# A trunk of four feed-forward layers and two mixers in split fp32: how the feed-forward groups leave the banks, and how the last layer begins its output rows

## The chip, the cores and the metric

The kernel runs on one core of a Trainium2 chip (trn2). The metric is the device time of one launch in microseconds (us); 2278.42 us is the median of three runs of the kernel before. The engines are TensorE (PE; its weight loads are PEld), VectorE (DVE), ScalarE (ACT), GpSimd (POOL) and SyncE (SP), which here only issues DMAs.

## The reference

A decoder trunk over x of 512 tokens by 1024 features, float32:

```
for i in range(2):
    x = x + 0.5 * rmsnorm(swiglu(rmsnorm(x, ng[0]), ffn1_w_in[i], ffn1_w_out[i]), ng[1])
    h = rmsnorm(x, ng[2])
    m = hgrn2(h, ...) if i == 0 else gated_deltanet(h, ...)
    x = x + rmsnorm(m, ng[3])
    x = x + 0.5 * rmsnorm(swiglu(rmsnorm(x, ng[4]), ffn2_w_in[i], ffn2_w_out[i]), ng[5])

def swiglu(x, w_in, w_out):
    gate, up = split(x @ w_in, 2)          # w_in 1024 x 5632
    return (silu(gate) * up) @ w_out       # w_out 2816 x 1024
```

The change touches the four SwiGLU layers alone.

## The kernel before

Six sections run one after the other on all engines: `ffn`, `hg`, `ffn`, `ffn`, `gd`, `ffn`; `s` is the section's number and `LAST - 1` the last. Every large product is made of three TensorE passes: each operand is split into a high part in fp32r (ScalarE's copy) and the low rest (VectorE's subtraction of the high part from the original), and high x high, high x low and low x high are added up in a bank of PSUM. A weight block of 128 x 1024 (a "unit", 512 KB) is loaded by SyncE's queue into `raw`, `raw_more` or `raw_last`, split into `w_hi` (L783 `split`, L855 `weights_high`) and `w_lo` (L1472, L1588 `weights_low`), each a ring of four units, and used. `lo_split` and `unit_used` count the units.

**The plain part of a feed-forward layer.** The first 6 of its 22 feature tiles (`PLAIN`) are six pairs of one gate and one up unit, features by tokens. `pair(n)` scales both out of their banks (L1550, L1554), ScalarE takes the SiLU (L840), GpSimd multiplies (L2273) into `y_all`. Meanwhile VectorE makes from x seven combined moving operands (`factor_raw`: `norm`, `sums`), which ScalarE and VectorE split into `factor` (L850, L1583 `factor_low`).

**The groups.** The other 16 tiles are four groups (`QUADS`) of four, done by a scheme with seven products of half size instead of eight: products 1, 2 (`gates_early`, `gates_end`), 6 (`join`), 5 (`step`), 7 (`diff`), 4 (`rest`), 3 (`ups_early`), each of 2 units x 2 token tiles x 2 x 3 = 24 matmuls (L2537), tokens by features. Weight blocks of 5, 6, 4 and 7 are sums and differences of loaded ones (`step_sum` L1592, `join_sum` L1597, `rest_sum` L1601, `diff_sum` L1604). TensorE's order is 1, (4 and 3 of the group before), 2, 6, (turn of the group before), 5, 7. Banks 0, 1 hold products 1 and then 2 on top (`SUM_BANKS`), 2, 3 product 6 (`JOIN_BANKS`), 4, 7 product 7 and then 4 on top (`DIFF_BANKS`), 5, 6 product 5 and then 3 on top (`UP_BANKS`).

ScalarE copies product 1 out (`keep_first`, L892) before product 2 may be added. VectorE adds: `joins` (L1610), `late_ups` (L1620, L1623), `late_gates` (L1630), `early_ups` (L1635). ScalarE takes two SiLUs (`first_silu` L901, `late_silu` L906). GpSimd multiplies (`late_product` L2278, `early_product` L2283). TensorE transposes the four row tiles back (`turn`, L2598) and ScalarE drains them into `y_all` (`drain`, L912).

**The end of a layer.** All 22 feature tiles of y are split into `act_hi` (ScalarE, L921 `act_high`, L926 `last_high`) and `act_lo`: the first twelve by GpSimd (`BY_POOL = 12`, L2287), the others by VectorE (L1640). The last four come straight out of the turn's banks. The output projection (L2458) then goes over the tiles; in the last section it is written with tokens in rows (`row_block`, L2636), a block of weights being one feature tile, 128 x 1024, and the last group's turn and all of VectorE's lows stand before its first matmul. Its first units wait for `late_silu`, then the load of the table set (L988), then `split`.

**The last section** also needs x with tokens in rows at the very end. VectorE transposes it in 32 x 32 blocks (`turn(chunks)`, L1646), in three portions between the pairs; SyncE's queue writes it out in 32 DMAs of 64 KB (L678) behind the loads of units 12 to 15, and the loads for the groups (L661, L668) stand behind those. `x_turned` lies where `y_all` has its last tiles, so `keep_first` of group 0 waits for `x_rows_stored` (L890).

VectorE, ScalarE, GpSimd and SyncE each work in the order written here; they meet TensorE through counting semaphores only. The waits the text speaks of:

```
pe.wait_ge(dve_rows, diff_added(s, q, t))                      # rest: L2555
pe.wait_ge(act_rows, first_kept(s, q, t))                      # gates_end: L2565
pe.wait_ge(pool_rows, y_early(s, q, 1))                        # turn: L2590
pe.wait_ge(act_ready, (ffn_no[s] + 1) * (KF - BY_POOL))        # last section: L2630
```

## Time and profile before

| | us |
|---|---|
| median of three runs (2277.6 to 2283.09) | 2278.42 |
| the profiled execution | 2279.39 |
| its span | 2277.7 |
| TensorE busy | 2211.7 |
| VectorE busy | 1571.3 |
| ScalarE busy | 1146.8 |
| GpSimd busy | 462.6 |
| mean granted TensorE clock | 0.990 |

The span is from the first to the last instruction; the execution's own time also has what lies around it. A busy TensorE is not TensorE at its peak, since matmuls overlap: what a matmul costs is read from the distance of the starts. In a timeline a row gives start, duration, engine, line, operation, out and in, the number of instructions merged, and in brackets the idle time before it and what ended it. Neighbouring instructions of an engine overlap by about 0.1 us, so their distance is a little less than their duration. The first feed-forward section is over at about 377 us, the second begins near 655, the third ends at 1375, the last begins near 1909.

### The profile page before, as it was taken

The numbers are of one execution on the slowest core, as the hardware profiler recorded it, in microseconds if no ns is written. First come the engines' busy times: TensorE is split into PE (matmuls) and PEld (weight loads), VectorE is DVE, ScalarE is ACT, GpSimd is POOL, SyncE is SP. The second block draws the span as 40 slices with busy tenths as digits, with TensorE's granted clock in tenths as the row PEclk, the third lists the DMA queues.
The fourth block names the chain that finished last, engine by engine and source line by source line (L and its number), as shares of the span: only waits on it lengthen the run. The fifth ranks groups of instructions, "written<-read, shape, count | busy, mean of one in ns | idle before, by whom it ended". The sixth has DMA issues, their size and how long they took to land.

```text
span 2277.7 us, 30876 instructions
## 1 busy us (share of the span) xinstructions
PE 2211.7 (97%) x11642; PEld 1826.0 (80%) x11642; DVE 1571.3 (69%) x1886; ACT 1146.8 (50%) x1655; POOL 462.6 (20%) x343
## 2 busy tenths in 40 slices
PE   9999999999999999999999999999999999999899
PEld 7787788788787887887887887877788788788687
DVE  6998536777568897358988338877666726898723
ACT  5456435555544455344456336476666724445412
POOL 3025200101101144001116010123721110012500
PEclk9999999999999999999999999999999999999899
DMA  5322332222223323323321332221122132532321
GB/s 172 125 88 68 104 102 93 66 87 79 71 78 122 101 74 91 96 91 111 129 93 51 109 86 91 85 83 57 57 66 75 57 105 80 135 125 75 129 93 65
DMA packets 84766, 208.57 MB, mean 92 GB/s; under 512 B 25088, under 2 KB 29312, under 8 KB 84640
## 3 DMA queue, kind: packets, MB, share of 16 engines
q1 hardware_dynamic: 84112, 206.59, 28.9%
q8 instruction: 84, 1.38, 0.2%
q14 instruction: 42, 0.34, 0.0%
q10 hardware_dynamic: 528, 0.26, 0.0%
HBM read 202.56 MB, written 4.26 MB: 91 GB/s over the span
## 4 chain that ended last, share of the span: by engine, by line
PE 76%; DVE 14%; ACT 3%; issue 3%; POOL 2%; DMA 1%; SPq 1%; DVEq 0%; ACTq 0%; POOLq 0%
PE bank L2458 36%; PE bank L2537 17%; PE bank L2857 9%; PE bank L2636 5%; DVE w_lo L1588 3%; DVE w_lo L1472 2%; DVE h_lo L1477 1%; DVE raw L1601 1%; ACT w_hi L783 1%; PE bank L2598 1%; SPq L678 1%; DVE raw_more L1604 1%; POOL act_lo L2287 1%; ACT h_hi L795 1%; DMA raw_more<-in_ffn_in 1%
## 5 line engine op out<-in xcount | busy, mean ns | idle before, releaser
L1472 DVE TENSOR_TENSOR w_lo<-raw,w_hi 128x1024 fp32r<-128x1024 f32 x283 | 362.4, 1293 | 434.4 <-ACT w_hi L783 434.3
L2537 PE MATMUL bank<-w_hi,factor 128*128 128x512 f32 x1792 | 557.9, 392 | 23.2 <-DVE w_lo L1588 12.4
L783 ACT ACTIVATE w_hi<-raw 128x1024 fp32r<-128x1024 f32 x283 | 293.9, 1054 | 285.1 <-PE bank L2458 188.8
L2537 PEld LDWEIGHTS bank<-w_hi,factor 128*128 128x128 f32 x1792 | 334.8, 189 | 101.7 <-issue 16.7
L2537 PE MATMUL bank<-w_lo,factor 128*128 128x512 f32 x896 | 350.0, 391 | 0.0
L2458 PE MATMUL bank<-h_hi,w_hi 128*128 128x512 f32 (+1 forms) x775 | 296.0, 382 | 7.8 <-DVE v_fm L1783 2.9
L2458 PE MATMUL bank<-h_hi,w_lo 128*128 128x512 f32 (+1 forms) x775 | 285.5, 368 | 0.0
L2458 PE MATMUL bank<-h_lo,w_hi 128*128 128x512 f32 (+1 forms) x748 | 275.3, 368 | 0.0
L2458 PE MATMUL bank<-act_hi,w_hi 128*128 128x512 f32 (+1 forms) x594 | 218.3, 367 | 5.2 <-DVE w_lo L1472 5.2
L2458 PE MATMUL bank<-act_hi,w_lo 128*128 128x512 f32 (+1 forms) x594 | 217.2, 366 | 0.0
L2458 PE MATMUL bank<-act_lo,w_hi 128*128 128x512 f32 (+1 forms) x594 | 217.1, 365 | 0.0
L2537 PEld LDWEIGHTS bank<-w_lo,factor 128*128 128x128 f32 x896 | 168.8, 188 | 35.8
L2458 PEld LDWEIGHTS bank<-h_hi,w_hi 128*128 128x128 f32 x775 | 146.6, 189 | 39.4 <-issue 8.5
L2458 PEld LDWEIGHTS bank<-h_hi,w_lo 128*128 128x128 f32 x775 | 146.6, 189 | 24.7
L2458 PEld LDWEIGHTS bank<-h_lo,w_hi 128*128 128x128 f32 x748 | 141.7, 189 | 24.6 <-issue 2.6
L2857 PE MATMUL bank<-h_hi,w_hi 128*128 128x512 f32 x360 | 150.9, 419 | 1.2 <-DVE conv_in L1883 0.7
L2857 PE MATMUL bank<-h_hi,w_lo 128*128 128x512 f32 x360 | 148.7, 413 | 0.0
L2857 PE MATMUL bank<-h_lo,w_hi 128*128 128x512 f32 x360 | 148.0, 411 | 0.0
L2458 PEld LDWEIGHTS bank<-act_hi,w_hi 128*128 128x128 f32 x594 | 112.1, 189 | 24.4 <-DVE w_lo L1472 6.4
L2458 PEld LDWEIGHTS bank<-act_lo,w_hi 128*128 128x128 f32 x594 | 112.1, 189 | 18.1
L2458 PEld LDWEIGHTS bank<-act_hi,w_lo 128*128 128x128 f32 x594 | 112.0, 189 | 18.1
L855 ACT ACTIVATE w_hi<-raw_more 128x1024 fp32r<-128x1024 f32 x80 | 84.8, 1060 | 73.5 <-PE bank L2537 36.8
(358 smaller groups left out, 4019.8 us busy)
## 6 DMA issues: line engine op xcount, KB each, us to landing
raw<-in_ffn_in SPq DMA_DIRECT2D x84, 512.0 KB, 3.7
raw<-in_gd_in SPq DMA_DIRECT2D x49, 512.0 KB, 3.6
raw_more<-in_ffn_in SPq DMA_DIRECT2D x48, 512.0 KB, 3.8
raw_last<-in_ffn_in SPq DMA_DIRECT2D x40, 512.0 KB, 4.9
raw<-in_ffn_out SPq DMA_DIRECT2D x48, 384.0 KB, 3.1
raw<-in_hg_in SPq DMA_DIRECT2D x32, 512.0 KB, 3.7
raw<-in_ffn_out SPq DMA_DIRECT2D x48, 320.0 KB, 2.9
raw<-in_last_out SPq DMA_DIRECT2D x22, 512.0 KB, 3.6
```

The costliest lines, as they stand in the source:

```text
L678: sp.dma_start(dst[:, c], src[:, c]).then_inc(x_rows_stored, 16)
L783: nc.scalar.activation(w_hi[:, u[0] % RING, :], raw[:, u[0] % RING, :], ACT.Copy).then_inc(hi_split, 1)
L795: nc.scalar.activation(h_hi[:, c, half(h)], x[:, c, half(h)], ACT.Copy, scale=pre_gain(s, c)).then_inc(h_hi_ready, 1)
L855: nc.scalar.activation(w_hi[:, u % RING, :], place, ACT.Copy).then_inc(hi_split, 1)
L1472: nc.vector.tensor_tensor(w_lo[:, r, :], raw[:, r, :], w_hi[:, r, :].bitcast(f32), ALU.subtract).then_inc(lo_split, 1)
L1477: nc.vector.scalar_tensor_tensor(out=h_lo[:, c, half(h)], in0=x[:, c, half(h)], scalar=pre_gain(s, c), in1=h_hi[:, c, half(h)].bitcast(f32 ...
L1588: TT(w_lo[:, u % RING, :], place, w_hi[:, u % RING, :].bitcast(f32), ALU.subtract).then_inc(lo_split, 1)
L1601: TT(lower_gate_place(s, q, a), lower_gate_place(s, q, a), join_place(s, q, a), ALU.subtract).then_inc(joint_made, 1)
L2458: ins = nc.tensor.matmul(dst[:, half(h)], w, moving[ml][:, k, :][:, half(h)], start=first and n == 0 and (wl, ml) == (0, 0), stop=last and ...
L2537: ins = nc.tensor.matmul(bank[dst[t]][:], factor[:, 2 * i + ml, at:at + P], (w_hi, w_lo)[wl][:, u % RING, b * TOK:(b + 1) * TOK], start=st ...
L2636: ins = nc.tensor.matmul(bank[tok_bank(t, h)][:], (act_hi, act_lo)[ml][:, k, t * P:(t + 1) * P], (w_hi, w_lo)[wl][:, r, half_row(h)], star ...
L2857: ins = MM(bank[unit_bank(n)][:], (w_hi, w_lo)[wl][:, (u0 + n) % RING, k * P:(k + 1) * P], (h_hi, h_lo)[ml][:, k, :], start=x == 0, stop=x ...
```

## The change

- `y` of the plain tiles is split soon after it is made: ScalarE's `act_high` in the pairs and after `keep_first` of group 0, the lows (`act_low`) by VectorE between its pairs and groups. GpSimd makes no lows. `ActHighs` and `ActLows` find each tile's place.
- The turned tiles of group 2 are split out of the banks (`turned_high`, `turned_low`) and no longer drained; those of group 3 as before.
- Product 4 goes into banks 2, 3 as a product of its own and waits for `joins`; `late_ups` writes its first sum to `late_gate`, where `late_gates` adds product 4.
- Product 1 of group 0 runs both units for token tile 0, then both for tile 1; `keep_first` copies tile 0 after the first half.
- VectorE's factor lows 2 to 6 move: 2 behind `pair(5)`, 3 between the two w_lo of product 6, 4 before w_lo(7,0), 5 and 6 behind w_lo(7,1).
- The last group's early product is VectorE's (`last_rows`).
- Last section: x is transposed before `pair(0)`, stored between the loads of units 11 and 12; the wait for the stores stands in `drain` of group 0. The output rows begin with token tile 2 for the first four weight blocks, then comes the turn, then tiles 0, 1 and 3 of the same blocks.

The diff's core (counters that only number the new order, and the SBUF layout, are left out):

```diff
 SyncE, last section
-                for n in range(0 if s else RING, N_PLAIN):
+                for n in range(0 if s else RING, 2 * PLAIN):
                     load((u0 + n, 0), weights(row0 + n))
                 if s == LAST - 1:
-                    for a in range(P // SUB):
-                        sp.wait_ge(turned, KD)
...
+                    for c in range(KD):
+                        sp.wait_ge(turned, c + 1)
+                        for a in range(P // SUB):
...
                             sp.dma_start(dst[:, c], src[:, c]).then_inc(x_rows_stored, 16)
+                for n in range(2 * PLAIN, N_PLAIN):
+                    load((u0 + n, 0), weights(row0 + n))
 ScalarE
 (pair)
+                    if n:
+                        act_high(n - 1)
 (keep_first)
-                    act.wait_ge(unit_used, unit_of(s, q, 1) + 2)
                     if q:
+                        act.wait_ge(unit_used, unit_of(s, q, 1) + 2)
                         act.wait_ge(dve_rows, join_made(s, q - 1, 1))
-                    elif s == LAST - 1:
-                        act.wait_ge(x_rows_stored, 16 * 4 * KD)
+                    else:
+                        act.wait_ge(y_turned, first_halves(s))
                     for t in range(2):
+                        if t and q == 0:
+                            act.wait_ge(unit_used, unit_of(s, q, 1) + 2)
 (drain)
+                    if s == LAST - 1 and q == 0 and fs[0] == 0:
+                        act.wait_ge(x_rows_stored, 16 * 4 * KD)
+                def turned_high(q, f):
+                    last = q == QUADS - 1
+                    act.wait_ge(unit_used, unit_of(s, QUADS - 1, 4 if last else 2) + 2)
+                    act.wait_ge(y_turned, turned_by(s, q, f))
+                    src = bank[(*DIFF_BANKS, *(JOIN_BANKS if last else SUM_BANKS))[f]]
+                    nc.scalar.activation(high_rows(PLAIN + 4 * q + f), src[:], ACT.Copy).then_inc(act_hi_ready, 1)
 (groups)
                     diff_weights(q, 0)
                     if last:
+                        turned_high(q - 1, 0)
+                        turned_high(q - 1, 1)
...
                     diff_weights(q, 1)
+                    if last:
+                        turned_high(q - 1, 2)
+                        turned_high(q - 1, 3)
...
-                for k in range(5, 10):
+                for k in range(PLAIN, PLAIN + 2):
                     act_high(k)
                 rest_weights(q, 0)
...
 VectorE
-                        TT(late_rows(t), bank[DIFF_BANKS[t]][:], sq[:, t, :], ALU.add).then_inc(dve_rows, 1)
+                        TT(late_gate(t), bank[DIFF_BANKS[t]][:], sq[:, t, :], ALU.add).then_inc(dve_rows, 1)
...
-                        TT(late_gate(t), bank[DIFF_BANKS[t]][:], sq[:, t, :], ALU.add).then_inc(dve_rows, 1)
+                        TT(late_gate(t), bank[JOIN_BANKS[t]][:], late_gate(t), ALU.add).then_inc(dve_rows, 1)
+                def last_rows():
+                    for t in range(2):
+                        dve.wait_ge(dve_rows, up_early(s, QUADS - 1, t))
+                        dve.wait_ge(act_rows, silu_first(s, QUADS - 1, t))
+                        TT(y_first[:, t, :], y_first[:, t, :], y[:, t, :], ALU.mult).then_inc(dve_rows, 1)
+                def turned_low(q, f):
+                    k = PLAIN + 4 * q + f
+                    src = bank[(*DIFF_BANKS, *(JOIN_BANKS if q == QUADS - 1 else SUM_BANKS))[f]]
+                    dve.wait_ge(act_hi_ready, act_count(s, k))
+                    TT(low_rows(k), src[:], high_rows(k).bitcast(f32), ALU.subtract).then_inc(act_ready, 1)
+                if s == LAST - 1:
+                    dve.wait_ge(x_ready, N_ITEMS * s)
+                    dve.wait_ge(acc_done, POOLED * (2 * s + 1))
+                    for c in range(KD):
+                        nc.vector.transpose(x_turned[:, c, :], x[:, c, :]).then_inc(turned, 1)
...
                     sums()
+                act_low(0)
                 pair(4, 0)
                 factor_low(0)
                 factor_low(1)
+                act_low(1)
+                pair(5, 2)
                 factor_low(2)
-                pair(5, 2)
 (group q, from w_lo(6,0) on)
                     weights_low(q, 6, 0, join_place(s, q, 0))
                     if q:
                         early_ups(q - 1)
+                    else:
+                        factor_low(3)
                     weights_low(q, 6, 1, join_place(s, q, 1))
...
                     weights_low(q, 5, 1, gate_place(s, q, 1))
                     if q == 0:
-                        for i in range(4, FACTORS):
-                            factor_low(i)
+                        factor_low(4)
+                    else:
+                        act_low(q + 2)
                     weights_low(q, 7, 0, up_place(0))
-                    joins(q)
+                    if last:
+                        turned_low(q - 1, 0)
+                        turned_low(q - 1, 1)
+                    if q:
+                        joins(q)
                     weights_low(q, 7, 1, up_place(1))
+                    if q == 0:
+                        factor_low(5)
+                        factor_low(6)
+                        joins(0)
+                        act_low(2)
                 q = QUADS - 1
+                turned_low(q - 1, 2)
+                turned_low(q - 1, 3)
                 weights_low(q, 4, 0, lower_gate_place(s, q, 0))
+                weights_low(q, 4, 1, lower_gate_place(s, q, 1))
                 late_ups(q)
-                weights_low(q, 4, 1, lower_gate_place(s, q, 1))
-                act_low(BY_POOL)
                 weights_low(q, 3, 0, lower_up_place(s, q, 0))
                 weights_low(q, 3, 1, lower_up_place(s, q, 1))
-                act_low(BY_POOL + 1)
+                for k in range(PLAIN, PLAIN + 4):
+                    act_low(k)
                 late_gates(q)
-                act_low(BY_POOL + 2)
-                act_low(BY_POOL + 3)
+                act_low(PLAIN + 4)
+                act_low(PLAIN + 5)
                 split((v0, 0))
+                act_low(PLAIN + 6)
+                act_low(PLAIN + 7)
                 early_ups(q)
                 split((v0 + 1, 0))
-                act_low(BY_POOL + 4)
-                act_low(BY_POOL + 5)
+                last_rows()
                 split((v0 + 2, 0))
                 split((v0 + 3, 0))
-                for k in range(KF - 4, KF):
-                    act_low(k)
+                for f in range(4):
+                    turned_low(q, f)
 GpSimd
-                for k in range(BY_POOL):
-                    act_low(k)
                 for t in range(2):
                     late_product(QUADS - 1, t)
-                for t in range(2):
-                    early_product(QUADS - 1, t)
 TensorE
 (product)
+                    if (q, p) == (0, 1):
+                        quarter(0, 0)
+                        quarter(1, 0).then_inc(y_turned, 1)
+                        for a in range(2):
+                            quarter(a, 1).then_inc(unit_used, 1)
+                        return
 (rest)
-                        pe.wait_ge(dve_rows, diff_added(s, q, t))
-                    product(q, 4, DIFF_BANKS, free, False)
+                        pe.wait_ge(dve_rows, join_made(s, q, t))
+                    product(q, 4, JOIN_BANKS, free, True)
 (diff, free)
+                        if q == QUADS - 1:
+                            pe.wait_ge(act_ready, act_count(s, KF - 8 + t))
 (last section)
-                turn(QUADS - 1)
-                pe.wait_ge(act_ready, (ffn_no[s] + 1) * (KF - BY_POOL))
-                for k in range(KF - RING):
+                for k in range(RING):
+                    pe.wait_ge(lo_split, v0 + k + 1 + SKEW)
+                    ready(k)
+                    for h in range(2):
+                        row_block(k, 2, h)
+                turn(QUADS - 1)
+                for t in range(2):
+                    pe.wait_ge(dve_rows, up_early(s, QUADS - 1, t))
+                    pe.wait_ge(act_ready, act_count(s, KF - 4 + t))
+                    for k in range(RING):
+                        for h in range(2):
+                            row_block(k, t, h)
+                pe.wait_ge(act_ready, act_count(s, KF - 1))
+                for k in range(RING):
+                    for h in range(2):
+                        ins = row_block(k, 3, h)
+                    ins.then_inc(unit_used, 1)
+                for k in range(RING, KF - RING):
```

## Rows read from the trace of the kernel before

**Rows 1.** The page's first part: busy us (share), instructions.

```profile
PE 2211.7 (97%) x11642; PEld 1826.0 (80%) x11642; DVE 1571.3 (69%) x1886; ACT 1146.8 (50%) x1655; POOL 462.6 (20%) x343
```

**Rows 2.** The chain that ended last, in order of time: start, us, what.

```profile
98.28 32.89 PE bank L2537 x144
```

**Rows 3.** TensorE's waits: total us, times, longest.

```profile
PE bank L2537 <- DVE w_lo L1588: 12.4, 16, 1.1
PE bank L2458 <- DVE w_lo L1472: 6.6, 7, 1.7
PE bank L2598 <- POOL y_first L2283: 6.0, 1, 6.0
PE bank L2537 <- ACT y_all L892: 6.0, 4, 3.7
PE bank L2537 <- DVE gate L1620: 3.7, 4, 0.9
```

**Rows 4.** Timeline of TensorE, first section's last group.

```profile
212.40 0.70 PE L2537 MATMUL bank<-w_hi,factor 128*128 128x512 f32 x2
...
216.21 0.73 PE L2537 MATMUL bank<-w_hi,factor 128*128 128x512 f32 x2 [0.80 <-DVE w_lo L1588]
...
225.59 0.70 PE L2537 MATMUL bank<-w_hi,factor 128*128 128x512 f32 x2 [0.93 <-DVE gate L1620]
...
232.94 0.73 PE L2537 MATMUL bank<-w_hi,factor 128*128 128x512 f32 x2 [0.92 <-DVE w_lo L1588]
...
240.40 0.50 PE L2458 MATMUL bank<-act_hi,w_hi 128*128 128x512 f32 x1 [1.72 <-DVE w_lo L1472]
```

**Rows 5.** Timeline of VectorE, same stretch.

```profile
213.84 4.55 DVE L1588 TENSOR_TENSOR w_lo<-raw_more,w_hi 128x1024 fp32r<-128x1024 f32 x2
218.32 1.28 DVE L1610 TENSOR_TENSOR sq<-bank,y_all 128x512 f32<-128x512 f32 x2
...
234.54 0.68 DVE L1630 TENSOR_TENSOR acc<-bank,sq 128x512 f32<-128x512 f32 x1
```

**Rows 6.** Timeline of GpSimd, same stretch.

```profile
208.33 23.47 POOL L2287 TENSOR_TENSOR act_lo<-y_all,act_hi 128x512 fp32r<-128x512 f32 x12
```

**Rows 7.** Timeline of ScalarE, same stretch.

```profile
236.50 1.28 ACT L988 ACT_TABLE_LOAD   x1
```

**Rows 8.** Timeline of VectorE, section at 655: groups 0 and 1.

```profile
728.37 1.22 DVE L1588 TENSOR_TENSOR w_lo<-raw,w_hi 128x1024 fp32r<-128x1024 f32 x1
...
731.77 3.50 DVE L1583 TENSOR_TENSOR factor<-factor_raw,factor 128x1024 fp32r<-128x1024 f32 x3
...
767.96 1.21 DVE L1588 TENSOR_TENSOR w_lo<-raw_more,w_hi 128x1024 fp32r<-128x1024 f32 x1
```

**Rows 9.** Timeline of TensorE, section at 655, group 0.

```profile
719.00 0.70 PE L2537 MATMUL bank<-w_hi,factor 128*128 128x512 f32 x2 [0.78 <-ACT y_all L892]
...
736.55 0.69 PE L2537 MATMUL bank<-w_hi,factor 128*128 128x512 f32 x2 [0.95 <-DVE w_lo L1588]
```

**Rows 10.** Timeline of SyncE's queue, last section.

```profile
1953.57 19.64 SPq L678 DMA_DIRECT2D x_rows<-x_turned  x32
```

**Rows 11.** Timeline of TensorE, last section, group 0.

```profile
1975.43 1.19 PE L2537 MATMUL bank<-w_hi,factor 128*128 128x512 f32 x2 [3.66 <-ACT y_all L892]
...
1997.34 0.70 PE L2537 MATMUL bank<-w_hi,factor 128*128 128x512 f32 x2 [1.11 <-DVE w_lo L1588]
```

**Rows 12.** Timeline of VectorE, last section, pairs.

```profile
1927.59 0.69 DVE L1550 TENSOR_TENSOR gate<-bank,rms 128x512 f32<-128x512 f32 x1 [0.45 <-ACT rms L790]
...
1935.78 1.89 DVE L1646 STREAM_TRANSPOSE x_turned<-resid 128x512 f32<-128x512 f32 x3
```

**Rows 13.** Timeline of TensorE, last section: turn and first rows.

```profile
2143.80 0.66 PE L2598 MATMUL bank<-ident,y_first 128*128 128x128 f32 x2 [6.03 <-POOL y_first L2283]
...
2149.53 0.79 PE L2636 MATMUL bank<-w_hi,act_hi 128*128 128x512 f32 x1 [2.08 <-DVE act_lo L1640]
```

**Rows 14.** Busy time by stretch: us, busy of each engine, TensorE's granted clock, DMA share, GB/s.

```profile
2149.50:2155.20 5.70, 5.67 (x14) 4.47 (x15) 0.00 (x0) 0.00 (x0) 0.00 (x0) 0.51 0.80 281
```

169 lines of the change are left out of this document (85 added, 84 removed).

## Prediction

> **What bounds the kernel now.** I read the page's first part, then TensorE's waits, then the timelines of each engine around the longest of these waits, and the chain that ended last for the pace. TensorE is busy for 97% of the span and nothing else comes near it [rows 1], so only its idle time and its slow stretches can be won: the change leaves every matmul in. The chain gives 144 matmuls of six products in 32.89 us [rows 2], so a product of 24 takes about 5.45 us, one matmul 0.227 us. TensorE's waits that concern the feed-forward code are five kinds, together 34.7 us (a few of the 6.6 us lie elsewhere) [rows 3]: a lower split of a weight block, the kept copy of the first product, an addition read out of the banks (`gate`, L1620), and in the last layer the turn behind GpSimd's `y_first`. The last layer also loses time with no wait: after 3.66 us of idleness, and again after the idle stretch before 2149.5, matmuls start at about half their rate; from 2149.5 to 2155.2 the granted clock is 0.51, the 1.2 GHz level, and 14 matmuls run where 25 would fit [rows 11, 14].
>
> The profiled execution took 2279.39 us (span 2277.7 and 1.7 around it), 1 us above the median 2278.42. I sum against 2279.39.
>
> **Closing stretch of a feed-forward layer (four times).** I take the first layer's; the others repeat it within 0.2 us. From the first matmul of the last group's product 5 at 212.40 to the first of the output projection at 240.40 pass 28.0 us, where four products need 21.8. The holes are before products' halves at 216.21, 225.59, 232.94 and at 240.40 [rows 4], with a smaller one between.
>
> Their cause is VectorE. While GpSimd computes, a 128x1024 subtraction of two SBUF operands takes 2.3 us; with GpSimd idle the same instruction takes 1.21 us, 1.13 from start to start [rows 5, 6, 8]. GpSimd's twelve `act_low` fill 23.5 us from 208.33 on [rows 6]. The change deletes them there. VectorE gets the twelve: at 0.60 us from start to start (the addition at 234.54, 0.68 with 0.08 of overlap [rows 5]; half of a 1.13 us one gives 0.57) that is 7.2 us, and 1.2 us for `last_rows`, which replaces the last `early_product`. Not all of it is in this stretch: lows 0 to 2 go into the pairs and group 0, lows 3, 4 and 5 into groups 1, 2 and 3. GpSimd's products for group 2 remain and run until 208.33, where the lows begin [rows 6], so relief starts there.
>
> I lay VectorE's new order out from that point, 1.13 for 1024 and 0.60 for 512 columns: diff sum 0 ends 208.9, w_lo(5,0) 210.0, diff sum 1 211.2, w_lo(5,1) 212.3, act_low(5) 212.9, w_lo(7,0) 214.0, two `turned_low` 215.2, joins 216.4, w_lo(7,1) 217.6, two `turned_low` 218.8, w_lo(4,0) 219.9, w_lo(4,1) 221.0. ScalarE must give the highs first: turn of group 2 begins at 210.7, so turned highs 0, 1 lie at 211.4 to 212.4, w_hi(7,1) 213.4, highs 2, 3 214.4; none is late. TensorE, from 212.5, wants (5,1) at 215.2, (7,0) 218.0, (7,1) 220.7, (4,0) 223.4, (4,1) 226.1: all are there, with 2.9 us or more in hand. So the hole at 216.21 goes. The fourth product writes bank 2, 3 and waits for the join additions (216.4), not for the additions that read banks 4 and 7, so the hole at 225.59 goes. Product 7 ends at 223.4; `late_ups` takes 2.4 us to 226.0, w_lo(3,0) 227.1, w_lo(3,1) 228.3, wanted at 228.9 and 231.6. The hole at 232.94 goes too. Product 3 ends at 234.3.
>
> What is late next: the output projection's first weight block. Its chain is late_gates, late_silu, the table load, w_hi, w_lo. Before, it took 5.86 us from 234.54 to 240.40 [rows 4, 5, 7]. It now starts when four act_lows (6 to 9) are done: 228.3 + 2.4 = 230.7, so the projection starts at 236.5 and TensorE waits 2.2 us for it. Gain 240.4 - 236.5 = 3.9 us. Its second block is wanted 4.1 us later, at 240.6; VectorE has two lows, `early_ups` and a split before it, 240.0. In three layers, 3 x 3.9 = **11.7 us**.
>
> The Trainium skill (SBUF — State Buffer, "Who interferes with whom") says that VectorE with two SBUF inputs contends with a GpSimd instruction that reads SBUF, one holding the port for its whole instruction, and that with one SBUF input it doesn't. By that rule alone the sum above holds and the rival "slower" below is out, while without it 2306 us stays possible. The trace agrees: the additions out of a bank at 218.32 take 0.6 us each while GpSimd works, and the 1024-wide ones before them twice their time [rows 5].
>
> **First group (four times).** The first product in order of token tiles lets ScalarE copy tile 0 2.7 us earlier, and gates_end no longer waits: 0.94 us at 719.00 [rows 9]. It is given back at once. Factor low 3 now stands before w_lo(6,1), so w_lo(5,0), which ended 729.6, ends 730.7 [rows 8], while TensorE (join held to 723.9 by w_lo(6,0)) is ready at 729.4: a new wait of 1.4 us. Product 5 then ends at 736.3. The wait at 736.55 [rows 9] goes, since one factor low stands before w_lo(7,0) instead of three (3.5 us) [rows 8]; it ends 735.3. Product 7 starts 736.35 instead of 736.55. Behind it stand factor lows 5, 6, the joins, act_low(2), then the next group's first w_lo at 741.6, wanted 741.8: just in time. Gain 0.2 us; bounds -1.2 (w_lo late by another instruction) and +2.0 (both holes gone). Four times: **0.6 us**, rounded down. The act_low in groups 1 and 2 cost nothing: there the block that it precedes is ready 4 us before TensorE wants it.
>
> **Last layer, first group.** Before, 32 stores of 64 KB took SyncE's queue 19.64 us from 1953.57, 0.61 each, and the kept copy waited for them to land [rows 3, 10]; the loads of up and lower_up stood behind them. From the first product (1975.43 - 3.8 - 5.45 = 1966.2) to product 7 at 1997.34 [rows 11] are 31.1 us; the layer at 719 needs 712.6 to 736.55, 23.9. So 7.2 us are lost, slow clock included. Now eight transposes (0.60 each from 1.89 for three, less overlap [rows 12], 4.8 in all) run before pair(0), and the 32 stores go from 1927.7 to about 1947.4, between load 11 and load 12. Loads 12 and 13 are wanted at 1959, 14 and 15 can't start before 1952 as now; the quarters find an empty queue. The wait for the stores moves to `drain`, 70 us later. The price: pair(0) starts at 1931.9 instead of 1927.59 [rows 12] (transposes can't begin before the gathers and splits end, 1927.1); gate, silu and gate again, 0.68, 0.7 and 0.7, make gate(1) ready at 1934.05; TensorE's unit 6 needs it and starts at 1966.2 - 6 x 5.45 = 1933.5, so it slips 0.6 us. Gain 7.2 - 0.6 = **6.6 us**.
>
> **Last layer, end.** Before, product 3 ended, TensorE idled 6.0 us to 2143.80 for y_first, turned at half clock, idled 2.08 us, and lost 5.7 x 0.49 = 2.7 us in the slow stretch behind 2149.5: as if the rows had begun at full speed at 2152.2 [rows 13, 14]. Now the shared part brings product 3's end to 234.3 + 1899.1 = 2133.4. Then four blocks of token tile 2, 1.36 us each, run as VectorE delivers them. In the first layer's times: block 0 at 236.5; w_lo 1 after two lows, early_ups and the split, 240.0; last_rows to 241.2; w_lo 2 242.3, w_lo 3 243.5. TensorE idles 2.2, 2.2 and 0.95 us, turns 245.2 to 247.0, and goes on with tile 0 after 0.1. Rows' full-speed equivalent: 234.3 + 5.35 + 1.75 + 0.4 = 241.8, that is 2140.9. Gain 2152.2 - 2140.9 = **11.3 us**.
>
> Sum: 11.7 + 0.6 + 6.6 + 11.3 = 30.2, so 2279.39 - 30.2 = **2249 us**.
>
> **Rivals.** *Clock.* The three idle stretches at the last layer's end lie between bursts of 1.36 us. After 3.66 us idle the clock fell to 1.2 GHz, after 1.72 us in the middle of work it didn't [rows 4, 11]; these are between. If it falls, the turn's 1.75 us may take half as long again and the slow stretch costs 2.7 [rows 14]: 2252.5. The Trainium skill (TensorE: Matmul & The Clock Gate, "What's actually happening") has the clock follow how busy the engine has recently been; this speaks against cutting the start into bursts.
>
> *Queues tie up.* turned_low waits for ScalarE, ScalarE for the turn, and w_lo(7,1) and w_lo(4,0) stand behind it. If turn or ScalarE is 3 us later than laid out, each layer gets back two holes of about 1 us, and the last layer's blocks 1 us: 2249 + 9 = 2258. Slack of 2.9 us speaks against it.
>
> *Stores do not hide.* They share the queue with loads 12 to 15; should those be late by as much as the stores took beyond my estimate, the 6.6 us are lost: 2256.
>
> *Slower.* GpSimd isn't what slows VectorE. Then the doubled times stay: nine and a half 1024-wide instructions of 1.13 us more and five lows of 1.2 more, less 2.5 us of slack, put late_gates 14.1 us later than laid out, so each layer's projection starts 14.1 - 3.9 = 10.2 us later than before. The last layer's own terms (6.6, and 11.3 - 3.9 = 7.4) remain: 2279.4 + 41 - 14 = 2306. Linear between the two, it decides once the instruction takes over 1.13 + 1.14 x 30.2 / 57 = 1.73 us. Against it: 1.21 us at 767.96, same line, with GpSimd idle [rows 8].
>
> **How the numbers follow.** As worked 0.55 (alone 2245 to 2253); clock 0.15; queues 0.13; stores 0.05; slower 0.04; the rest split: better than worked (first-group holes both gone) 0.06, none of it 0.02. The range 2242 to 2263 reaches from the better case, 4 x 1.8 us below, past queues and stores with some of both. 0.3% is 6.8 us, about what a measurement can tell. Faster 0.92, same 0.03, slower 0.05.
>
> **What would show it.** Right: VectorE's w_lo at 1.2 us in the last group; no hole in products 5, 7, 4, 3; 2.2 us before the projection; 1.4 us before product 5 of group 0; no 3.7 us wait near 1971; two or three waits under 2.5 us at L2636. Wrong: w_lo still at 2.3, waits inside products 4 or 3, or a clock of 0.5 at the rows' start.

## Result and the profile after

The kernel after takes 2256.27 us (median of 4 runs, 2255.43 to 2257.03) where the kernel before took 2278.01: the ratio is 0.990, 95% interval 0.9883 to 0.9917, 22 us less. 2249 was forecast; the time lies inside the range, 7 us above the forecast. The profiled executions are 2279.39 and 2256.88 us, 22.5 apart, and everything below is worked out between them.

The page's first part, for [rows 1]:

```profile
PE 2199.7 (98%) x11642; PEld 1819.9 (81%) x11642; DVE 1549.6 (69%) x1942; ACT 1139.2 (51%) x1639; POOL 366.1 (16%) x287
```

TensorE's waits (us in total, times, longest), for [rows 3]:

```profile
PE bank L2514 <- DVE w_lo L1515: 8.3, 7, 2.3
PE bank L2703 <- DVE w_lo L1515: 4.9, 3, 2.3
PE bank L2593 <- DVE w_lo L1631: 4.6, 4, 1.2
PE bank L2668 <- POOL y_first L2347: 4.1, 3, 1.4
PE bank L2593 <- issue: 3.9, 4, 1.1
```

The kept copy and `gate` are gone from the list, and the sixteen waits for weight lows inside products are four. New are `y_first` before the first turn three times, and four waits in the products for nothing the profile names, where before had one. The first section's timeline of TensorE, every hole over 0.15 us, and at 215.48 the first matmul of the last group's product 5, for [rows 4]:

```profile
87.46 0.70 PE L2593 MATMUL bank<-w_hi,factor 128*128 128x512 f32 x2 [0.93 <-issue]
...
94.32 0.70 PE L2593 MATMUL bank<-w_hi,factor 128*128 128x512 f32 x2 [1.13 <-DVE w_lo L1631]
...
134.03 0.41 PE L2668 MATMUL bank<-ident,y_first 128*128 128x128 f32 x2 [1.35 <-POOL y_first L2347]
...
215.48 0.71 PE L2593 MATMUL bank<-w_hi,factor 128*128 128x512 f32 x2
...
239.79 0.74 PE L2514 MATMUL bank<-act_lo,w_hi 128*128 128x512 f32 x2 [2.29 <-DVE w_lo L1515]
```

Between the last two lines lie products 5, 7, 4 and 3 without a hole, 24.3 us where [rows 4] had 28.0. A hole in this text is the distance of two starts less the 0.23 us of a matmul; the brackets, which count from a modelled end, show about 0.15 us less (2.29 for a hole of 2.44). The last section ends so, for [rows 13]:

```profile
2124.19 0.73 PE L2703 MATMUL bank<-w_hi,act_lo 128*128 128x512 f32 x2 [2.29 <-DVE w_lo L1515]
...
2127.72 0.73 PE L2703 MATMUL bank<-w_hi,act_lo 128*128 128x512 f32 x2 [1.88 <-DVE w_lo L1515]
...
2130.06 0.73 PE L2703 MATMUL bank<-w_hi,act_lo 128*128 128x512 f32 x2 [0.70 <-DVE w_lo L1515]
...
2135.08 0.70 PE L2703 MATMUL bank<-w_hi,act_lo 128*128 128x512 f32 x2 [0.25 <-DVE act_late L1692]
```

To compare kernels part by part I counted matmuls: a feed-forward section's grouped part is the same number of them in every kernel here, so the time from the start of one to the start of another can be set side by side. "Group 0" is the first 120, "to turn 0" the next 120 (group 1 up to its turn), "closing" the last 96 (products 5, 7, 4, 3) up to the first projection matmul. "Second series" is experiment 5. At 0.2266 us a matmul they would take 27.2, 27.2 and 21.8 us. The four columns of each are the four sections, us; where the last turn comes ahead of the rows (before, and last turn first), the last section's closing reaches up to that turn:

```
kernel (profiled run)   group 0                    to turn 0                  closing
before                  29.31 29.49 29.60 36.73    27.21 27.21 27.21 27.21    28.00 28.01 27.99 32.30
after                   29.83 29.95 29.71 29.95    28.71 27.23 28.75 28.73    24.31 24.31 24.31 24.33
after, second series    29.10 29.39 29.21 29.12    27.26 28.76 28.71 27.26    24.34 24.34 24.34 24.34
product 4's bank back   29.65 29.15 29.11 29.08    28.75 28.75 28.76 27.26    24.36 24.36 24.36 24.36
GpSimd busy             29.88 29.86 29.94 29.30    27.24 27.23 28.72 27.23    28.87 28.85 28.83 28.98
stores late             30.22 29.17 29.34 36.60    27.23 28.75 28.73 28.73    24.34 24.34 24.34 24.34
last turn first         29.14 29.15 29.16 29.08    27.26 28.72 27.26 27.26    24.31 24.34 24.34 29.17
products on VectorE     29.65 29.95 29.22 29.75    27.21 27.23 27.22 27.24    24.30 24.31 24.31 24.33
weights split early     29.79 29.74 29.10 29.18    27.25 27.23 28.73 27.24    21.89 21.86 21.89 21.89
group 0's order         27.20 27.25 27.20 28.24    27.21 27.21 27.21 27.26    24.34 24.31 24.31 24.34
all orders              27.20 27.21 27.65 28.27    27.21 27.21 27.24 27.22    21.89 21.86 21.86 21.89
all, and products       27.20 27.23 27.96 28.28    27.21 27.21 27.26 27.23    21.86 21.86 21.86 21.89
all, bank back          27.20 27.23 27.23 28.22    27.21 27.21 27.26 27.25    23.05 23.07 23.07 23.08
all, last rows' order   27.33 27.25 27.23 28.24    28.71 27.21 27.22 27.26    21.89 21.86 21.86 21.89
```

### The profile page after: what moved, and what is told of

Read it like the earlier page. It is cut to its first block, busy times and chain, and to the rows that moved or that the text cites. A ratio compares the mean times of both kernels' runs of the same rounds, so it can differ in the third digit from the quotient of the medians.

```text
span 2255.2 us, 30953 instructions
## 1 busy us (share of the span) xinstructions
PE 2199.7 (98%) x11642; PEld 1819.9 (81%) x11642; DVE 1549.6 (69%) x1942; ACT 1139.2 (51%) x1639; POOL 366.1 (16%) x287
## 3 DMA queue, kind: packets, MB, share of 16 engines
q1 hardware_dynamic: 84112, 206.59, 29.4%
## 4 chain that ended last, share of the span: by engine, by line
PE 78%; DVE 10%; issue 5%; ACT 3%; POOL 2%; DMA 2%; SPq 0%; DVEq 0%; ACTq 0%; POOLq 0%
PE bank L2514 37%; PE bank L2593 18%; PE bank L2941 9%; PE bank L2703 5%; DVE w_lo L1515 2%; DVE w_lo L1631 1%; PE bank L2668 1%; DMA raw_more<-in_ffn_in 1%; DVE h_lo L1520 1%; ACT w_hi L821 1%; ACT h_hi L833 1%; DVE resid L1550 1%; PE bank L3103 1%; PE bank L3082 1%; PE bank L3110 1%
## 5 line engine op out<-in xcount | busy, mean ns | idle before, releaser
L2514 PE MATMUL bank<-act_late,w_hi 128*128 128x512 f32 (+1 forms) x648 | 200.7, 367 | 0.0
L2514 PE MATMUL bank<-act_lo,w_hi 128*128 128x512 f32 (+1 forms) x540 | 171.2, 368 | 6.9 <-DVE w_lo L1515 6.9
L2514 PE MATMUL bank<-act_late,w_lo 128*128 128x512 f32 (+1 forms) x432 | 158.0, 366 | 0.0
L2514 PEld LDWEIGHTS bank<-act_late,w_hi 128*128 128x128 f32 x648 | 118.8, 189 | 19.7
L2514 PEld LDWEIGHTS bank<-act_lo,w_hi 128*128 128x128 f32 x540 | 100.0, 190 | 24.9 <-DVE w_lo L1515 8.1
L1631 DVE TENSOR_TENSOR w_lo<-raw_more,w_hi 128x1024 fp32r<-128x1024 f32 x80 | 100.5, 1268 | 20.6 <-ACT w_hi L895 20.6
```

The lines of the kernel that those rows point to most:

```text
L1631: TT(w_lo[:, u % RING, :], place, w_hi[:, u % RING, :].bitcast(f32), ALU.subtract).then_inc(lo_split, 1)
L2514: ins = nc.tensor.matmul(dst[:, half(h)], w, moving[ml][:, k, :][:, half(h)], start=first and n == 0 and (wl, ml) == (0, 0), stop=last and ...
```

## The experiments

Twelve runs, one of them the kernel after again; each edit is to the kernel after unless it says otherwise, and the cuts shown leave out what only follows from them. Experiments 1 to 4 are compared with 2256.27 us, experiments 6 to 10 with the second series' 2256.62, experiments 11 and 12 with experiment 9. The kernel before took 2278.5 us beside the second series and 2278.9 beside experiment 9.

**1. Product 4 back on the difference's banks.**

```diff
-                        pe.wait_ge(dve_rows, join_made(s, q, t))
-                    product(q, 4, JOIN_BANKS, free, True)
+                        pe.wait_ge(dve_rows, diff_added(s, q, t))
+                    product(q, 4, DIFF_BANKS, free, False)
...
-                            pe.wait_ge(dve_rows, gate_late(s, q - 1, t))
+                            pe.wait_ge(dve_rows, join_made(s, q - 1, t))
```

> The kernel after, with its fourth product put back on the difference's banks (product 4 adds onto what product 7 left in banks 4 and 7, and the join's product waits for the step before it as in the kernel before); all else stays. Theory (the bank of its own removes a wait of TensorE in the last group of each section, where product 4 stood ready and VectorE had not yet added the difference): the hole ahead of product 4 in the last group comes back at about 1.1 us in each of four sections, and the time is 2260.5, 4.2 us over the kernel after. Rival A (the hole had gone because VectorE is no longer slowed by GpSimd there, and the bank does nothing): within 1 us of the kernel after. Rival B (the additions of the difference now stand ahead of what joins wait for in every group, so that holes come in groups 2 and 3 too): 2265 or more.

2252.78 us (2251.17 to 2256.93), ratio 0.9885 (0.987 to 0.990). TensorE, at product 4 and at the projection:

```profile
226.45 0.70 PE L2595 MATMUL bank<-w_hi,factor 128*128 128x512 f32 x2 [0.93 <-DVE gate L1663]
...
238.72 0.73 PE L2516 MATMUL bank<-act_lo,w_hi 128*128 128x512 f32 x2 [1.12 <-DVE w_lo L1515]
```

The hole came back where the theory had it, and the projection's fell from 2.44 us to 1.28: the closing stretch is the same to 0.05 us. All three expectations missed the time. In the kernel after the bank only moves a microsecond, because the projection's first weight low ends when it ends.

**2. GpSimd kept busy in the last group.** 22 subtractions that nothing reads:

```diff
+                pool.wait_ge(dve_rows, gate_late(s, QUADS - 2, 1))
+                for n in range(22):
+                    pool.wait_ge(pool_rows, POOL_ROWS * ffn_no[s] + 18 + n)
+                    nc.gpsimd.tensor_tensor(idle_rows[:], x[:, 0, 0:2 * P], x[:, 1, 0:2 * P], ALU.subtract).then_inc(pool_rows, 1)
                 for t in range(2):
                     late_product(QUADS - 1, t)
```

> The kernel after, with GpSimd kept busy in the last group of each section: 22 subtractions of 128x256 that nothing reads, about where the kernel before had its twelve lows (some 20 us); they leave nothing out of the computation. Theory (in the kernel before it was GpSimd's traffic in SBUF that drew VectorE's weight lows from 1.2 to 2.3 us in this stretch, and VectorE's lateness that made TensorE wait): VectorE's instructions of 128x1024 on SBUF come back to about 2.3 us each while GpSimd runs, holes ahead of products 5, 7 and 4 come back, and the time is 2260 to 2262. Rival A (the lows' cost was the wait of the projection for GpSimd's own results, not its traffic): no change, within 1 us of 2256.3. Rival B (a 256 wide instruction gives VectorE its turn twice as often, so the slowing is half): VectorE's come to 1.6 to 1.8 us, holes under 0.5 us, 2257 to 2258.

2277.89 us (2274.82 to 2280.69): 21.6 us more, the whole gain of the change. GpSimd, VectorE and TensorE in the first section, then the stretch behind (us, busy time of each engine, granted clock):

```profile
208.13 29.40 POOL L2360 TENSOR_TENSOR idle_rows<-resid 128x256 f32<-128x256 f32 x22
```

```profile
210.68 1.76 DVE L1632 TENSOR_TENSOR w_lo<-raw_more,w_hi 128x1024 fp32r<-128x1024 f32 x1
```

```profile
242.01 0.80 PE L2519 MATMUL bank<-act_lo,w_hi 128*128 128x512 f32 x1 [5.91 <-DVE w_lo L1516]
```

```profile
242.00:246.00 4.00, 3.99 (x9) 3.14 (x10) 4.00 (x6) 1.22 (x2) 0.00 (x0) 0.50 0.34 98
```

VectorE's instructions go from 1.21 to 1.76 us, which is what rival B said of them (a narrower GpSimd instruction delays less than the 2.3 us beside one of 512), and the loss is far over the theory's: 4.5 us in each closing stretch, 18.3 in all, and TensorE's clock at its 1.2 GHz level behind the hole. My 4 to 6 us was the cost of one section. The load is also longer than the lows of before were (29.4 us, not 23.5), and late products queue behind it, so this isn't the old kernel. But VectorE has no idle stretch from 204.5 to 239.7 in the first section, so it is late by its slower instructions alone: GpSimd's traffic is enough to take the gain away. The prediction had put the point where nothing is left of the gain of the new order at 1.73 us an instruction; here it is 1.76.

**3. The last layer's stores late**, transposes in three portions, stores behind all loads, and the copy waiting for them, as before:

```diff
+                turn(range(0, 3))
                 pair(2, 5)
...
+                        if s == LAST - 1:
+                            act.wait_ge(x_rows_stored, 16 * 4 * KD)
```

> The kernel after, with the last layer's transposes of x and their stores as in the kernel before: transposes in three portions between the first pairs, the 32 stores on SP behind all its weight loads, and ScalarE's copy of the first product's result waiting for all of them. Theory (that chain was what held up the last layer's first group): a hole of about 7 us comes back in that group, the time is 2262.9, 6.6 us over the kernel after. Rival (the early transposes now cost nearly as much where they stand, ahead of the first pair, so undoing them gives half of it back): 2259 to 2260.

2261.22 us (2260.4 to 2261.87), 4.9 more. TensorE in the last section's group 0:

```profile
1966.30 0.70 PE L2599 MATMUL bank<-w_hi,factor 128*128 128x512 f32 x2 [3.36 <-ACT y_all L934]
...
1976.11 0.70 PE L2599 MATMUL bank<-w_hi,factor 128*128 128x512 f32 x2 [2.47 <-issue]
```

The median lies between the theory's 2262.9 and the rival's 2260; the stretch itself is clear. Group 0 goes from 29.95 to 36.60 us, 6.65 as the theory says; the second hole is the join, whose loads stood behind the stores. The 0.5 us ahead of the pairs comes off. The rest of the difference between 6.1 and 4.9 is of the size in which the second series of the kernel after differs from its first in group 0.

**4. The last turn first**, then all rows: `turn(QUADS - 1)` and a wait for all 22 lows ahead of the row blocks.

> The kernel after, with the last projection in the order of before: the last turn first, then a wait for all 22 highs and lows, then all rows tile by tile, instead of tile 2 of the first four rows ahead of the turn. Theory (the order hides the chain of product, turn, copy and low behind 16 row blocks): TensorE's idle time between its last product and steady rows grows from 5.6 us to 8.5 to 12, the time is 2259.1 if its clock doesn't fall and 2262.7 if it falls to half for a stretch. Rival (the chain isn't hidden in the kernel after either, its holes of 2.44, 2.04, 0.86 and 0.30 us being the same chain in parts): within 1 us of 2256.3.

2260.35 us (2252.88 to 2261.59), 4.1 more.

```profile
2124.76 0.66 PE L2668 MATMUL bank<-ident,y_first 128*128 128x128 f32 x2 [7.12 <-DVE y_first L1682]
...
2129.84 0.73 PE L2703 MATMUL bank<-w_hi,act_lo 128*128 128x512 f32 x2 [1.47 <-DVE act_late L1692]
```

Two holes of 7.28 and 1.62 us in place of 5.64 in four: the new order of the rows is worth 3.3 us of holes, as the theory says. With the clock, which fell to its 1.2 GHz level at 2121.4 here, it is 4.5: the last section takes 159.8 us from the last group's product 5 to the end, not 155.3. The medians alone don't show it, as the two intervals overlap (ratio 0.9895 to 0.9924 here, 0.9883 to 0.9917 for the kernel after).

**5. The kernel after again.**

> The kernel after itself, unchanged, timed beside the next three kernels on their chip. It says how far a few holes of 1 us and a few falls of TensorE's clock carry a kernel from one series to another. Theory (the kernel with product 4 back on the difference's banks was no faster than the kernel after, its 3.5 us being startup and clock falls that come in some executions and not in others): the ratio to before lies between 0.9885 and 0.9905, the time at 2254 to 2257. Rival (the bank of its own costs time): 2256.3 again, ratio 0.990 or more.

2256.62 us (2255.05 to 2258.29), ratio 0.9904 (0.9888 to 0.992). Both expectations hold this result, so it doesn't choose between them. The interval overlaps that of experiment 1, so whether the shared bank is 3 us better in this kernel stays undecided; experiment 11 asks it again where it can be seen. The table shows what changes from one execution to the next: group 0 by up to 0.8 us, and the turn's 1.5 us, which is there in other sections now.

**6. GpSimd's products of groups 0 to 2 on VectorE.**

```diff
                     weights_low(q, 6, 1, join_place(s, q, 1))
+                    if q:
+                        products(q - 1)
                     rest_sum(q, 0)
```

> The kernel after, with the twelve products of gate and up rows per section that GpSimd did in groups 0 to 2 on VectorE (4 more instructions of 128x512 in SBUF in a group, some 0.68 us each by VectorE's low of that size), in the place behind the low of the join's second quarter. Theory (the hole of 1.5 us ahead of the first group's turn comes from GpSimd and VectorE competing for SBUF, which starves one of them): all turn holes go (3 to 4 of them, 1.5 us each, 4.6 to 6 us), no VectorE instruction of 128x1024 in groups 1 to 3 takes over 1.3 us, and the time is 2251. Rival A (VectorE is full there, and its four more products push the lows that TensorE waits for): holes of 1 to 2 us ahead of product 5 or 7 in nine groups, 2260 or more. Rival B (the turn waits for the products wherever they are made, as they depend on the silu of the late gates): the holes stay at 1 to 1.5 us, 2256.

2251.95 us (2247.47 to 2254.04), 4.7 less: all four runs lie below those of the second series, the turn's hole is gone from all four sections, and closing and group 0 don't move. GpSimd in the kernel after, first section and third (at 709), then VectorE beside the first:

```profile
120.84 2.60 POOL L2342 TENSOR_TENSOR gate<-acc,gate 128x512 f32<-128x512 f32 x1 [42.18 <-ACT acc L948]
123.39 8.04 POOL L2342 TENSOR_TENSOR up<-rms,up 128x512 f32<-128x512 f32 x1
131.38 2.51 POOL L2347 TENSOR_TENSOR y_first<-y,y_first 128x512 f32<-128x512 f32 x2
...
755.71 2.28 POOL L2342 TENSOR_TENSOR up<-rms,up 128x512 f32<-128x512 f32 x1
757.94 4.59 POOL L2347 TENSOR_TENSOR y_first<-y,y_first 128x512 f32<-128x512 f32 x2
```

```profile
123.39 1.21 DVE L1631 TENSOR_TENSOR w_lo<-raw,w_hi 128x1024 fp32r<-128x1024 f32 x1
124.52 2.34 DVE L1644 TENSOR_TENSOR raw_last<-raw_last,raw 128x1024 f32<-128x1024 f32 x2
126.79 1.21 DVE L1647 TENSOR_TENSOR raw_more<-raw,raw_more 128x1024 f32<-128x1024 f32 x1
127.93 1.21 DVE L1631 TENSOR_TENSOR w_lo<-raw_more,w_hi 128x1024 fp32r<-128x1024 f32 x1
129.06 1.21 DVE L1647 TENSOR_TENSOR raw_more<-raw,raw_more 128x1024 f32<-128x1024 f32 x1
```

The same product takes 2.28 us or 8.04. In the long case VectorE runs at full speed, and GpSimd's product ends at 131.43, 1.2 us behind VectorE's string: about its own time, as if it had got nowhere before; in the short one they take turns, and VectorE's two sums take 4.54 us. The kernel after, run again, has the long case in the section at 709, where it was short:

```profile
756.44 8.04 POOL L2342 TENSOR_TENSOR up<-rms,up 128x512 f32<-128x512 f32 x1
```

**7. The projection's first weights split early.** On ScalarE the high goes ahead of the silus:

```diff
+                v0 = u0 + IN_UNITS["ffn"]
+                split((v0, 0))
                 late_silu(q)
                 act.preload_act_table_set("natural_log_exp_and_others")
```

On VectorE lows 6 to 8 go ahead of `late_ups`, and low 9 and the split ahead of `late_gates`.

> The kernel after, with the projection's first weights split earlier at each section's end: ScalarE makes the high of the first out unit ahead of the late silus and the table load (where it stood idle 6.2 us), VectorE makes its low ahead of the late gates, and takes three of the four lows 6 to 9 into its idle 2 us ahead of the late ups. Theory (the hole of 2.44 us ahead of the projection is the chain late gates, silu, silu, table load, high, low, in that order on two engines): the hole falls to under 0.8 us in each of four sections, and the time is 2249, 6.5 to 7 us less. Rival A (the first unit is ready but the second isn't, so the hole comes one unit later): about 1 us of it stays behind the first unit's blocks, 2252. Rival B (in the last section the turn is put back by what ScalarE does first): its holes of 2.04 and 0.86 us grow by 1, 2250 to 2252.

2243.77 us (2238.45 to 2245.38), 12.8 less. VectorE:

```profile
229.41 1.22 DVE L1516 TENSOR_TENSOR w_lo<-raw,w_hi 128x1024 fp32r<-128x1024 f32 x1
230.55 0.68 DVE L1672 TENSOR_TENSOR acc<-bank,acc 128x512 f32<-128x512 f32 x1
231.15 0.68 DVE L1672 TENSOR_TENSOR rms<-bank,rms 128x512 f32<-128x512 f32 x1
231.75 4.69 DVE L1687 TENSOR_TENSOR act_lo<-y_all,act_late 128x512 fp32r<-128x512 f32 x4
```

Closing is 21.9 us, what its matmuls take; 2.45 us four times is 9.8. The theory had 6.5 to 7 and was too low. The 3 us beyond the holes aren't taken apart; falls of TensorE's clock are a part that the traces show. Behind a wait of 2.45 us ahead of the projection the clock fell to its 1.2 GHz level in 8 of 18 cases (the first three sections of the six profiled runs that have this wait), at 1.4 to 1.6 us each, and in none of the 15 where the wait is gone. In the last section a hole of 2.69 us is left at the second row, as rival A said for the second unit. The four lows now run beside GpSimd's late products and take 4.69 us instead of 2.49.

**8. Group 0's order:** factor lows 2 and 3 ahead of the last pair, both `up` quarters loaded ahead of the `lower_up` ones.

> The kernel after, with two orders changed in each section's first group: VectorE makes the lows of factors 2 and 3 ahead of the last plain pair (where it stood idle 3.2 us), and SP loads up quarters 0 and 1 ahead of lower up quarters 0 and 1. Theory (the hole of 1.0 to 1.2 us ahead of the join's product comes from the sum that waits 0.6 us for the second up quarter to land and the factor low ahead of it, the hole of 1.3 us ahead of product 5 from the factor low between the lows): both go, 2.3 us in each of four sections (the last section's first hole was 0.5), and the time is 2248. Rival A (the lower up quarters, now later, hold up the join's sum instead): only the second hole goes, 2251. Rival B (the pair's own up row is now late by a factor low): 2254.

2246.85 us (2244.41 to 2251.28), 9.8 less. Group 0 is 27.2 us in three sections, its matmuls' own time, 28.2 in the last. VectorE's sums no longer wait for a load; in the kernel after the second one did:

```profile
82.64 1.23 DVE L1635 TENSOR_TENSOR raw<-raw_more,raw 128x1024 f32<-128x1024 f32 x1 [0.63 <-DMA raw_more<-in_ffn_in]
```

**9 and 10. All three orders together**, with the second unit's split early too; then the same with experiment 6's products.

> The kernel after, with the order of the first group (factor lows and up quarters earlier) and the early split together, and the second unit's high and low early too, ahead of the late silus on ScalarE and of the lows 10 to 13 on VectorE; GpSimd keeps its products. Theory (the holes are separate, so their gains add up): those of the first group 9.2 us (four sections at 2.3), those ahead of the projection 9.8 us (four at 2.44, the last section too now), one fall of TensorE's clock less (1.5 us): 2237 to 2238. Rival A (a hole closed ahead only moves to the next wait, as product 4's did): at most the better of the two, 2243.8. Rival B (the second unit's split ahead of the silus puts the last turn back): the last section keeps some 2.5 us of holes, 2239 to 2240.

> The kernel before this one in the series (all three orders), with the twelve products of GpSimd per section on VectorE too. Theory (the hole ahead of the turn comes by the phase in which GpSimd's up product meets VectorE's string of SBUF instructions, 8.03 us instead of 2.28, in 1 to 3 of the sections of an execution): it can't come any more, 1.5 to 4 us, 2234 to 2236, and the runs spread less. Rival (the orders have moved the phase so that GpSimd is never starved, and VectorE's four more products per group cost): no change or up to 2 us slower, 2237 to 2240.

2233.86 us (2233.11 to 2235.89), ratio 0.981 (0.9796 to 0.9823), and 2234.31 (2230.8 to 2234.66). The gains add up, 12.8 + 9.8 to 22.8. That is more than the 2237 to 2238 of the theory. The first three sections have no hole left in their grouped part but 0.4 us. VectorE's products give nothing more: the long case was in no section of the profile of experiment 9.

**11. All orders, product 4's bank back.**

> The kernel with all three orders and GpSimd's products (2233.9 us, no hole over 0.15 us in the first four feed-forward sections), with product 4 back on the difference's banks. Theory (the bank of its own removes a wait of 1.09 us ahead of product 4, and in the kernel after that microsecond was given back ahead of the projection, because the projection waited for a chain that does not start from product 4's wait but from its own engines' order; with that chain gone the bank is worth what it removes): holes of 1.09 us ahead of product 4 in the last group of four sections, the time is 2238.2, 4.4 us more. Rival A (now the hole ahead of product 4 gives the other engines time, and smaller holes behind it fall away): 2235 to 2236. Rival B (as in the kernel after, no difference): 2233.9.

2239.29 us (2238.49 to 2240.13), 5.4 more than experiment 9, the runs apart, on the same chip. Closing is 1.2 us longer in each section, and the hole stands at product 4:

```profile
223.44 0.70 PE L2594 MATMUL bank<-w_hi,factor 128*128 128x512 f32 x2 [0.93 <-DVE gate L1662]
```

So the bank is worth 4.8 us of four holes, once nothing behind takes them back.

**12. The last rows' order on VectorE.** In the last section its lows of rows 3 and 4 go ahead of `last_rows` and lows 11 to 13.

> The kernel with all three orders, and in the last section VectorE's order changed once more: the lows of the third and fourth out rows' weights stand ahead of the products of the last early rows and of the activations' lows 11 to 13, which come behind them. Theory (the hole of 3.66 us at the third row and the 1.2 us lost with TensorE's clock at half behind it are VectorE's order alone: its low came at 2103.9 while its high was there at 2098.8): both go, 4 to 5 us, the time is 2229 to 2230. Rival A (the turn then waits for the products of the last early rows): a hole of 1 to 2 us ahead of the turn, 2231 to 2232. Rival B (GpSimd's two late products slow these lows as they slowed the lows 10 to 12): half of the hole stays, 2231.5.

2232.33 us (2229.78 to 2232.85), ratio 0.9794 (0.978 to 0.9809), 1.5 less. TensorE in experiment 9, then VectorE in this one:

```profile
2105.15 0.73 PE L2702 MATMUL bank<-w_hi,act_lo 128*128 128x512 f32 x2 [3.50 <-DVE w_lo L1514]
```

```profile
2102.98 1.99 DVE L1514 TENSOR_TENSOR w_lo<-raw,w_hi 128x1024 fp32r<-128x1024 f32 x1 [0.25 <-ACT w_hi L818]
```

The 3.66 us hole became 0.42 and the clock stayed up, 4.8 us in that stretch. The profiled run gave 1.5 of it back to a turn in the first section (28.71 in the table) and more to the clock elsewhere, so the median shows a third of it. It is the fastest of the kernels here, though its interval overlaps that of experiment 9.

## Why the prediction came out 7 us short

By its own terms, the profiled execution of before against that of the kernel after, and against that of the second series:

```
term                                          predicted   measured   second series
closing stretch, three sections                    11.7       11.1            11.0
first group, sections 1 to 3                        0.6       -1.1             0.7
last layer, first group                             6.6        6.2             7.0
last layer, end                                    11.3       10.9             9.7
the turn behind GpSimd's products                     0       -4.6            -3.2
rest of the program                                   0        0.0            -2.2
sum                                                30.2       22.5            23.0
```

The measured ones are differences of the table's columns; the end of the last layer runs from the last group's product 5 to the end of the program, 166.2 us before and 155.3 after. The forecast 0.6 was meant for all four first groups. The last layer's first group is 36.73 - 29.95 = 6.8, less a new hole of 0.5 in the pairs where 0.6 was forecast.

**Closing stretch: right, mechanism and size.** VectorE's 1024-wide instructions are at 1.21 us, all holes inside the products are gone, and what was to be late next was late: the projection, 2.44 us against 2.2. "Slower", that GpSimd isn't what slows VectorE, is out by experiment 2. One part of the account was wrong in its reason: I let the hole at 225.59 go to the new bank as a gain. Experiments 1 and 11 show that the bank is worth nothing as long as ScalarE and VectorE reach the projection's first weights last, and 1.2 us a section when they don't.

**The turn: the step that failed.** I took over groups 1 to 3 with "the act_low in groups 1 and 2 cost nothing", and priced the contention in one direction: GpSimd makes VectorE's instruction twice as long. It has another outcome, in which GpSimd is held for 8.04 us and the turn waits for its products. That cost 1.5 us in three sections of the profiled run, and two in the next series. Experiment 6 takes it away by taking GpSimd out, with 4.7 us of the median. No section of before has it, of 28 sections with the kernel after's group 0 and GpSimd's products 14 have it, of 16 with the new order in group 0 one, and the same kernel has it and hasn't it in the same place.

It goes with how the two engines first meet, at GpSimd's `gate` just ahead of `up`. The kernel after, at 709 (short), then in the first section (long, its `gate` is the row at 120.84 in experiment 6):

```profile
754.33 1.42 POOL L2342 TENSOR_TENSOR gate<-acc,gate 128x512 f32<-128x512 f32 x1 [42.33 <-ACT acc L948]
754.51 2.31 DVE L1631 TENSOR_TENSOR w_lo<-raw,w_hi 128x1024 fp32r<-128x1024 f32 x1
```

```profile
121.05 1.21 DVE L1631 TENSOR_TENSOR w_lo<-raw,w_hi 128x1024 fp32r<-128x1024 f32 x1
```

`gate` starts 0.18 us ahead of VectorE's next instruction in the short case and makes it wait; it starts 0.21 us ahead in the long one, and waits itself, 2.60 us in place of 1.42. All 48 sections with GpSimd's products sort this way: the 33 short ones lead by 0.17 to 0.20 us, the 15 long ones by 0.20 to 0.25, but for one of 0.19. What moves the start by these hundredths stays open; no run sets it directly.

**First group: mis-sized in the profiled run, -0.4 us a section instead of +0.2.** In the second series it is +0.2, so the size lies within what one kernel's executions differ by, and there is only one trace of before. The forecast wait of 1.4 us ahead of product 5 is there, 1.29 us. What I sized too small is the join, which I had held to 723.9, about 0.4 us of waiting: with the first product's copy out of the way, TensorE reaches it early and waits 1.0 to 1.2 us (0.4 to 0.7 in the second series), as VectorE's second sum waits for its quarter to land and the factor low stood ahead of it (the row in experiment 8). Experiment 8 took both holes away by two swaps in the first three sections. "Given back at once" was right, but it was given back for want of an order, not of work.

**Last layer, first group: right.** Experiment 3 brings 6.65 us back in the place. "Stores do not hide" is out.

**Last layer, end: right in sum.** Holes of 2.44, 2.04 and 0.86 us for 2.2, 2.2 and 0.95. The *clock* rival didn't come there in the profiled run of the kernel after; in the second series the same holes brought the 1.2 GHz level. The Trainium skill (TensorE: Matmul & The Clock Gate, "What's actually happening") has the gate follow how busy the engine has recently been. The traces agree so far: behind the four waits of 6.0 to 6.7 us behind the last product in experiment 2 the clock fell each time, behind the three of 1.9 us in before never. Between them it isn't settled by the wait alone: behind the same wait of 2.9 us near 411, before ran at the low level and after didn't (stretch, busy times, granted clock; before first):

```profile
411.10:417.90 6.80, 5.97 (x17) 4.90 (x18) 0.68 (x2) 0.00 (x0) 0.00 (x0) 0.51 0.24 77
```

```profile
411.10:417.90 6.80, 6.45 (x31) 5.47 (x32) 2.07 (x6) 1.21 (x2) 0.00 (x0) 1.00 0.19 69
```

**Rest of the program.** Its zero is a sum: 3.2 us won between 240 and 640 by a clock that didn't fall, 1.4 lost behind the projection's wait near 1230 where it did, 1.0 lost at the start, 0.8 in smaller pieces. The start doesn't belong to the change: ten of the thirteen profiled runs with it reach group 0 within 0.2 us of before. The 1.4 us may: the change made the wait ahead of the projection longer, from 1.9 us to 2.45, and behind 2.45 the clock fell in 8 of 18 cases, behind 1.9 in none of three. The prediction had a fall of the clock only in the last layer.

**Queues tie up** didn't come: the turned lows were on time and no product in the last group waits.

## What to carry to other kernels

A hole that is closed shows what it was worth only when nothing behind it ends at a fixed time: follow the chain of the next wait first, and ask whether it starts from the hole or from another engine's own order. Look for idle time of the helping engines just ahead of each chain: here three reorderings without any less work gave as much again (23 us) as the whole change. And where GpSimd and VectorE work in SBUF side by side, price both sides: each of them can be the one that waits.

## What the runs showed of the hardware

A GpSimd product of 128x512 takes 1.27 us by itself at the end of a section, 2.28 when it takes turns with VectorE, and 8.04 in the other outcome, where VectorE's string of 1024-wide subtractions goes on undelayed. VectorE's own instruction is then 1.21 us, 1.76 beside GpSimd instructions of 256 columns, and 2.3 beside those of 512. The Trainium skill (SBUF — State Buffer, "Who interferes with whom") describes the shared port as an exclusive lock; that the delay grows with the other's width agrees with it, and the 8.04 us shows that the turns needn't be fair. Which engine loses went with 0.03 us in how far ahead of VectorE's next instruction GpSimd started.

A wait of TensorE of 2.45 us ahead of the projection was followed by its 1.2 GHz level in 8 of 18 cases, at 1.4 to 1.6 us each; 6.0 us were followed by it three times in three, at up to 2.8 us. Whether it comes can differ in the same place of the same kernel: the kernel after kept its clock near 411, 608 and 2124 in one profiled execution and lost it in the other, which cost about 3.4 us in all. That is the largest of three parts by which these two executions differ; the first groups make 2.6 the other way and the turns 1.4.
